# The large mixtures of a two-network kernel: experts' rows combined in SBUF by a 0/1 matrix, shared weights loaded in halves

## The chip, the core and the metric

The kernel runs on one core of a Trainium2 chip. The metric is the device time of one execution in microseconds; lower is better. TensorE, VectorE (DVE), ScalarE (ACT), GpSimd (POOL) and the sync engine (SP) run instruction streams of their own and wait for each other on semaphores; 16 DMA engines move data between HBM and SBUF.

## What is computed

512 tokens of 1024 features pass through three blocks, each a mixer and a mixture of experts. The first mixture has 16 experts (MoE0). The second and third (MoE1, MoE2) are the large ones: 64 experts with weights of 1024x256, 1024x256 and 256x1024 in f32, of which each token uses two, and a shared expert of width 512 for all tokens:

```python
def hier_moe(h, w_rg, b_rg, w_re, b_re, w_gate, w_up, w_down, ws_gate, ws_up, ws_down, w_sg):
    """Top-1 group, then top-2 experts inside the group; plus gated shared expert."""
    ...
    gate = jax.nn.softmax(top_v, axis=-1) * p_sel[:, None]
    eid = g_sel[:, None] * EXPERTS_PER_GROUP_2 + top_i
    ...
        hid = jax.nn.silu(xb @ w_gate[e]) * (xb @ w_up[e])
        return hid @ w_down[e]
    ...
    y = jnp.zeros((N, D), xt.dtype).at[tok_sorted].add(out[dest] * gate_sorted[:, None])
    ys = (jax.nn.silu(xt @ ws_gate) * (xt @ ws_up)) @ ws_down
    y = y + jax.nn.sigmoid(xt @ w_sg) * ys
```

Behind it stands `x = x + gt2 * rmsnorm(y, ...)`, and then the next mixer or the output.

## The kernel before

The program is written engine by engine in stages: MoE0, a convolution mixer, MoE1, a gated delta network (gdn), MoE2. A mixture is `moe_sp`, `moe_pe`, `moe_ve`, `moe_ac` and `moe_gp`, one function for each engine, and the order in them is the order on the engine.

**Units.** A large mixture does 16 units (`m.NS`) of 4 experts with 32 rows each, 128 rows in all; up to 8 further units take the overflow of experts with more than 32 tokens (`overflow`, with branches on a count). In this run MoE1 has no overflow unit and MoE2 one. For unit n: `gather_gp` fetches the tokens' rows from `xn_d` in HBM; `turn_pe` transposes them (8 transposes), `turn_ve`/`turn_ac` write them to SBUF with the modulation; `gate_up_pe` multiplies by gate and up weights (64 matmuls of 256 columns, 128 records in the trace); `hidden_pe` transposes the product; `down_pe` multiplies by the down weights (16 matmuls of 512 columns). `down_ve` and `down_ac` copy a half each to `YB`, and ScalarE's queue stores the 128 rows of 4 KB to `y_d` in HBM (L2005). After the last unit GpSimd gathers each token's two rows from `y_d` (8 gathers, L2105), and `mix` scales and adds them to the shared expert's output `SO`.

**The loop on TensorE** for n = 0 to 15: gate and up of unit n, hidden of n-1, transposes of n+1, down of n-1, then `m.rate` = 2 side steps (`next(more)`) of the shared expert: 4 matmuls of 128x512 a step.

**The loads.** SP's queue issues all weight loads (L295), 1 MB each, into slots: 0 to 7 are the ring, 8 to 14 lie in the arena. A load waits until what was in its slot is used. The order in the loop is down of n-1, gate of n+1, up of n+1, four loads each, so each group of four waits for the group two ahead of it in the ring. A down load waits for gate weights (`("ps", "gu", ...)`), an up load for down weights. At a mixture's start 14 slots are filled ahead; the third load, of the shared gate weights, waits in slot 8 for the projection before the mixture (`m.after`), and with it all behind it.

**Positions.** While VectorE routes (`route_ve`), TensorE does two small steps for it, `positions_pe` and `tokens_pe`, and then waits for the first gather.

## Time and profile before

| | |
|---|---|
| runs of the kernel before | 2825.89, 2830.32, 2833.78 us; median 2830.32 |
| span of the profiled execution | 2829.8 us |
| busy share: PE, PEld, DVE, ACT, POOL | 75%, 53%, 38%, 29%, 8% |
| loads on q1 | 625.04 MB, 59.1% of 16 engines |
| ACT's queue, q10 | 37.23 MB, 3.2% |
| row stores to `y_d` | 51 of 512 KB, median 8.5 us from issue to landing |
| gathers from `y_d` | 24 |
| MoE1 streams, MoE2 streams | about 1176 to 1676 us, 2268 to 2775 us |

The page gives one execution: busy time of each engine, the span in 40 slices with the granted TensorE clock and the transfer rate, the DMA queues, the chain that ended last, and the costliest groups of instructions. A stage is read from its own slices, since the shares are means over stages with different bounds. A TensorE record with "128*32 128x256" has 32 weight columns and a moving operand of 256 columns; one f32 matmul leaves two records. "second" is a tile of type fp32r, "ring" and "arena" hold f32. In a timeline the brackets say how long the engine had been idle and what ended that.

### The profile page before, as it was taken

To read this page: it belongs to the slowest core of one execution; us is meant where nothing else is said; L and a number is where in the kernel's file an instruction comes from. 1 tells how busy PE (TensorE), PEld (TensorE's weight loads), DVE (VectorE), ACT (ScalarE), POOL (GpSimd) and SP (SyncE) were. 2 spreads that over 40 slices of the span, in tenths; PEclk is the share of its full clock that TensorE was granted. 3 is DMA by queue.
4 is the path that set the end of the run, shared out by engine and by line. 5 is a ranking of instruction groups with operands and counts; after the bars stand their busy time and mean duration, and the time that the engine had idled before them with its cause. 6 is when DMAs were issued, how large, how long until landed. Compare 5 with 4: busy or idle time off the path is not lost. (4 is left out here: it accounts for less than half of the span.)

```text
span 2829.8 us, 41468 instructions
## 1 busy us (share of the span) xinstructions
PE 2130.7 (75%) x17466; PEld 1499.7 (53%) x17466; DVE 1081.7 (38%) x1714; ACT 821.3 (29%) x1345; POOL 214.9 (8%) x220
## 2 busy tenths in 40 slices
PE   5999998897994799576766545899988676667652
PEld 3877776795773688332333214677766532323221
DVE  3278877544223444410111016566545520011103
ACT  4177776322223423200000005344423310100101
POOL 2001000101101000100000000111110100000001
PEclk8999999988997899788888777999998798888776
DMA  8357765546983222899999983211112699999995
GB/s 312 126 191 235 237 225 194 79 156 206 335 322 138 94 91 79 350 412 394 412 413 409 413 315 115 60 46 41 44 46 75 235 401 412 413 413 415 403 404 210
DMA packets 218816, 698.20 MB, mean 247 GB/s; under 512 B 24365, under 2 KB 123382, under 8 KB 161782
## 3 DMA queue, kind: packets, MB, share of 16 engines
q1 hardware_dynamic: 195446, 625.04, 59.1%
q0 software_dynamic: 12992, 33.10, 3.4%
q10 hardware_dynamic: 10176, 37.23, 3.2%
q8 instruction: 144, 2.36, 0.3%
q14 instruction: 58, 0.48, 0.0%
HBM read 664.34 MB, written 45.11 MB: 251 GB/s over the span
## 5 line engine op out<-in xcount | busy, mean ns | idle before, releaser
L220 PE MATMUL PS<-ring,arena 128*32 128x256 f32 (+5 forms) x7488 | 797.8, 486 | 408.7 <-DMA ring<-in_moe_w_up 172.7
L220 PE MATMUL PS<-second 128*128 128x256 f32 (+1 forms) x4416 | 798.8, 340 | 34.3 <-DVE second L239 28.6
L220 PEld LDWEIGHTS PS<-ring,arena 128*32 128x32 f32 (+3 forms) x7488 | 413.4, 138 | 749.6 <-issue 585.8
L220 PEld LDWEIGHTS PS<-second 128*128 128x128 f32 x4416 | 671.5, 194 | 143.9 <-issue 30.5
L232 ACT ACTIVATE arena<-PS 128x512 f32<-128x512 f32 (+1 forms) x338 | 170.3, 504 | 1038.2 <-PE PS L220 889.8
L239 DVE TENSOR_TENSOR arena<-arena,PS 128x256 f32<-128x256 f32 (+1 forms) x83 | 43.5, 524 | 746.5 <-PE PS L220 745.5
L220 PE MATMUL PS<-arena 128*64 128x64 f32 (+8 forms) x1600 | 270.2, 358 | 36.1 <-DVE arena L239 17.2
L258 DVE COPY arena<-PS 128x512 f32<-128x512 f32 (+4 forms) x169 | 93.6, 554 | 391.7 <-PE PS L220 367.1
L220 PEld LDWEIGHTS PS<-arena 128*128 128x128 f32 (+5 forms) x1600 | 156.4, 168 | 154.8 <-issue 106.1
L232 ACT ACTIVATE arena<-PS,small 128x128 f32<-128x128 f32 (+1 forms) x212 | 99.6, 470 | 458.8 <-PE PS L228 451.4
L228 PE MATMUL PS<-ident,arena 128*128 128x128 f32 x919 | 133.6, 296 | 130.5 <-ACT arena L232 79.2
L232 ACT ACTIVATE arena<-arena 128x512 f32<-128x512 f32 (+5 forms) x239 | 169.0, 707 | 166.3 <-DVE arena L239 59.3
L239 DVE TENSOR_TENSOR second<-ring,second 128x1024 fp32r<-128x1024 f32 (+1 forms) x88 | 142.6, 1621 | 192.4 <-ACT second L232 187.4
L228 PEld LDWEIGHTS PS<-ident,arena 128*128 128x128 f32 x919 | 112.3, 152 | 162.3 <-ACT arena L232 81.9
L239 DVE TENSOR_TENSOR arena<-arena 128x512 f32<-128x512 f32 (+10 forms) x286 | 176.3, 616 | 34.1 <-ACT arena L232 16.7
L232 ACT ACTIVATE second<-ring 128x1024 fp32r<-128x1024 f32 (+1 forms) x88 | 120.5, 1370 | 214.6 <-PE PS L220 193.2
L2084 POOL DMA_INDIRECT arena<-xn_d,arena x51 | 52.8, 1035 | 960.0 <-PE PS L228 753.9
L246 DVE TENSOR_SCALAR arena<-PS,small 128x128 f32<-128x128 f32 (+1 forms) x212 | 87.9, 415 | 35.4 <-PE PS L228 26.8
L220 PE MATMUL PS<-ring 64*64 64x64 f32 (+3 forms) x1792 | 76.7, 232 | 11.6 <-DVE ring L239 9.4
L220 PEld LDWEIGHTS PS<-ring 64*64 64x64 f32 (+2 forms) x1792 | 70.3, 143 | 24.0 <-DVE ring L239 14.1
L266 POOL TENSOR_TENSOR arena<-arena 128x768 f32<-128x768 f32 (+2 forms) x31 | 47.6, 1535 | 385.0 <-DVE arena L246 236.2
L2105 POOL DMA_INDIRECT arena<-y_d,arena x24 | 26.4, 1100 | 375.5 <-ACTq L77 369.1
(158 smaller groups left out, 1105.9 us busy)
## 6 DMA issues: line engine op xcount, KB each, us to landing
ring<-in_moe_w_up SPq DMA_DIRECT2D x148, 1024.0 KB, 12.2
ring<-in_moe_w_down SPq DMA_DIRECT2D x148, 1024.0 KB, 11.1
ring<-in_moe_w_gate SPq DMA_DIRECT2D x142, 1024.0 KB, 11.0
ring<-in_ada_w SPq DMA_DIRECT2D x48, 1024.0 KB, 5.4
y_d<-arena ACTq DMA_DIRECT2D x51, 512.0 KB, 8.5
ring<-in_w_mod SPq DMA_DIRECT2D x24, 1024.0 KB, 6.3
ring<-in_gdn_in_w SPq DMA_DIRECT2D x32, 512.0 KB, 4.1
ring<-in_hg_w_in SPq DMA_DIRECT2D x24, 512.0 KB, 7.2
```

What stands on the lines that cost most here:

```text
L220: return P.e.matmul(o, l, r, start=st, stop=sp)
L228: return P.e.transpose(o, i, ident[:, :])
L232: A.e.activation(o, i, f, **kw).then_inc(*A.mark(*label))
L239: V.e.tensor_tensor(o, a, b, op).then_inc(*V.mark(*label))
L246: V.e.tensor_scalar(o, a, s1, s2, op0, op1).then_inc(*V.mark(*label))
L258: V.e.tensor_copy(o, a).then_inc(*V.mark(*label))
L266: G.e.tensor_tensor(o, a, b, op).then_inc(*G.mark(*label))
L2084: G.e.indirect_dma_start(out=XG[n % 3][0:m.G_ * m.C], out_offset=None, in_=xn_d, in_offset=bass.IndirectOffsetOnAxis(ap=m.idx[0:m.G_ * m.C ...
L2105: G.e.indirect_dma_start(out=m.ybuf[i], out_offset=None, in_=m.y_d, in_offset=bass.IndirectOffsetOnAxis(ap=m.yi[:, i // 2, i % 2:i % 2 + 1 ...
```

## The change

For MoE1 and MoE2 alone:

- `down_ac` scales unit n's rows by the tokens' gate values `m.ws` into `YP[0]`, rounded to fp32r; `down_ve` writes what the rounding left into `YP[1]`. `where_ve` makes the 0/1 matrix `WT`, rows to tokens. `combine_pe` multiplies both by it: 4 token tiles x 2 halves x 2 = 16 matmuls of 128x512. `combine_ve` adds the eight results to `XN` in SBUF (unit 0 copies). The side steps of the shared expert's down product add to `XN` too.
- The stores to `y_d`, the eight gathers behind the last unit, `mix` and the zero fill of 4 MB of `y_d` at the program's start go.
- `m.ws` and the token numbers come from more small work in routing (`shares_ve`, `shares_pe`, `columns_ve`).
- The shared gate and up weights come in eight halves of 0.5 MB each through slots 15 and 16. Four side steps stand ahead of the first unit; then a loop has one, loops 1, 3, 5 and 12 two. MoE1's ring starts at slot 0.
- Transposes of n+1 stand behind down of n-1. PSUM banks: six for units (0 to 4 and 7), 5 and 6 for the side steps.

```diff
-        for ne, c_, p in ((16, 128, 128), (64, 32, 128)):
+        for ne, c_, p in ((16, 128, 128),):
...
+    YP = [second[AR0 + 23040][:, 1024 * i:1024 * i + 1024] for i in range(2)]
+    WT = second[AR0 + 29184][:, :]
...
+    def piece_sp(m, q):
+
+        p, w, h = q // 4, q // 2 % 2, q % 2
+        src = m.shared[w][:, 256 * p:256 * p + 256].rearrange("(p h k) n -> p h k n", h=2, k=4)[:, h]
+        load(slots(15 + h), src, 4, ("ps", "sh", m.i, p, w, h), "sh", m.i, p, w, h, n=1024)
...
+    def begin_sp(m, turn):
+
+        free = ("ps", "cv", 11, 1) if m.i == 1 else ("ps", "rc", 7, 1)
+        state["slots"].update({12: free, 13: free, 14: ("sq2", m.before, 3), 15: m.after, 16: m.after, 9: None, 10: None})
+        expert_sp(m, slots(12), 0, 0, 0)
+        expert_sp(m, slots(13), 0, 0, 1)
+        for w, h in ((0, 2), (0, 3), (1, 0), (1, 1)):
+            expert_sp(m, turn, 0, w, h)
+        for q in range(2):
+            piece_sp(m, q)
+        for n, w, h in ((0, 1, 2), (0, 1, 3), (1, 0, 0), (1, 0, 1)):
+            expert_sp(m, turn, n, w, h)
+        S.wait_ge(at("xn_d", m.i), at("ps", "h2T", m.i, 3, 1))
+        expert_sp(m, slots(9), 1, 0, 2)
+        expert_sp(m, slots(10), 1, 0, 3)
+        expert_sp(m, slots(14), 1, 1, 0)
+        for q in range(2, 4):
+            piece_sp(m, q)
+        for h in range(1, 4):
+            expert_sp(m, turn, 1, 1, h)
...
         for n in range(m.NS):
+            if m.shared and n in (2, 3, 4, 6):
+                piece_sp(m, {2: 4, 3: 5, 4: 6, 6: 7}[n])
+            if m.shared and n in (5, 9):
+                if n == 5:
+                    state["slots"][11] = ("tokf2", m.i)
+                else:
+                    state["slots"][8] = ("ps", "sh", m.i, 1, 1, 1)
+                shared_down_sp(m, n // 9)
             if n:
...
-        S.wait_ge(at("comb", m.i, 7))
+        if m.shared:
+            S.wait_ge(at("ps", "cm", m.i, m.NB - 1, 3, 1))
...
+    def combine_pe(m, n):
+
+        P.wait_ge(at("W", m.i, n), at("ev", "down", m.i, n, 1))
+        for t in range(4):
+            for f in range(2):
+                b = take(state["units"], "cm", m.i, n, t, f)
+                for j in range(2):
+                    i = mm(b, WT[:, 128 * t:128 * t + 128], YP[j][:, 512 * f:512 * f + 512], j == 0, j == 1)
+                i.then_inc(*P.mark("ps", "cm", m.i, n, t, f))
...
-            for f in range(2):
-                for w in range(2):
-                    b, u = take(turn, "sh", m.i, p, f, w), unit("sh", m.i, p, w)
-                    P.wait_ge(at("ld", "sh", m.i, p, w))
-                    for k in range(8):
-                        P.wait_ge(at("h2", m.i, k))
-                        i = mm(b, u[:, k, f * 128:(f + 1) * 128], H2T[:, k, :], k == 0, k == 7)
-                        if k == 3:
-                            yield
-                    i.then_inc(*P.mark("ps", "sh", m.i, p, f, w))
-                    yield
+            for w in range(2):
+                b2 = [take(turn, "sh", m.i, p, w, f) for f in range(2)]
+                for h in range(2):
+                    u = unit("sh", m.i, p, w, h, k=4, n=1024)
+                    P.wait_ge(at("ld", "sh", m.i, p, w, h))
+                    for f, b in enumerate(b2):
+                        for k in range(4):
+                            P.wait_ge(at("h2", m.i, 4 * h + k))
+                            i = mm(b, u[:, k, f * 128:(f + 1) * 128], H2T[:, 4 * h + k, :], h + k == 0, h == 1 and k == 3)
+                        if f:
+                            i.then_inc(*P.mark("ps", "sh", m.i, p, w, h))
+                        yield
...
         more = shared_pe(m) if m.shared else iter(())
+        next(more, None)
         positions_pe(m)
+        next(more, None)
         tokens_pe(m, "tok", 0, m.NS)
+        for _ in range(2):
+            next(more, None)
         turn_pe(m, 0)
         for n in range(m.NS):
             gate_up_pe(m, n)
+            if m.shared and n == 0:
+                shares_pe(m, "share", m.NS)
             if n:
                 hidden_pe(m, n - 1)
-            if n + 1 < m.NS:
+            if m.shared is None and n + 1 < m.NS:
                 turn_pe(m, n + 1)
             if n:
                 down_pe(m, n - 1)
-            for _ in range(m.rate):
+            if m.shared and n + 1 < m.NS:
+                turn_pe(m, n + 1)
+            if m.shared and n:
+                combine_pe(m, n - 1)
+            for _ in range(side_steps(n)):
                 next(more, None)
             if n == 1:
                 tokens_pe(m, "tok2", m.NS, m.NB)
+                if m.shared:
+                    shares_pe(m, "share2", m.NV)
...
+        if m.shared:
+            combine_pe(m, m.NS - 1)
...
+        if m.shared:
+            for f in range(2):
+                V.wait_ge(at("ps", "down", m.i, n), at("hi", "y", m.i, n, f))
+                stt(YP[1][:, 512 * f:512 * f + 512], bank("down", m.i, n, f), m.ws[:, n:n + 1], YP[0][:, 512 * f:512 * f + 512].bitcast(f32),
+                    ALU.mult, ALU.subtract, "ev", "down", m.i, n, f)
+            return
...
+    def where_ve(m, n):
+
+        V.wait_ge(at("ps", "cm", m.i, n - 1, 3, 1) if n else None)
+        tt(WT.rearrange("p (t s) -> p t s", s=128), bc(iota[:, :].unsqueeze(1), 4, 128), bc(m.tokf[:, n, :].unsqueeze(2), 4, 128), ALU.is_equal, "W", m.i, n)
+
+    def combine_ve(m, n):
+
+        for t in range(4):
+            for f in range(2):
+                o, b = XN[:, t, 512 * f:512 * f + 512], bank("cm", m.i, n, t, f)
+                V.wait_ge(at("ps", "cm", m.i, n, t, f))
+                if n:
+                    tt(o, b, o, ALU.add, "ev", "cm", m.i, n, t, f)
+                else:
+                    cp(o, b, "ev", "cm", m.i, n, t, f)
...
             for n in range(2):
+                o = XN[:, t, n * 512:(n + 1) * 512]
                 V.wait_ge(at("ps", "sd", m.i, t, n))
-                ts(SO[:, t, n * 512:(n + 1) * 512], bank("sd", m.i, t, n), m.sgate[:, t:t + 1], None, ALU.mult, None, "ev", "sd", m.i, t, n)
+                stt(o, bank("sd", m.i, t, n), m.sgate[:, t:t + 1], o, ALU.mult, ALU.add, "ev", "sd", m.i, t, n)
...
             if n:
                 hidden_ve(m, n - 1)
-            if n + 1 < m.NS:
+            if m.shared is None and n + 1 < m.NS:
                 turn_ve(m, n + 1)
             if n:
                 down_ve(m, n - 1)
+            if m.shared and n + 1 < m.NS:
+                turn_ve(m, n + 1)
+            if m.shared and n:
+                combine_ve(m, n - 1)
+                where_ve(m, n)
...
+        if m.shared:
+            for f in range(2):
+                A.wait_ge(at("ps", "down", m.i, n), at("ps", "cm", m.i, n - 1, 3, 1) if n else at("ev", "share", m.i), at("ev", "share2", m.i) if n >= m.NS else None)
+                act(YP[0][:, 512 * f:512 * f + 512], bank("down", m.i, n, f), ACT.Copy, "hi", "y", m.i, n, f, scale=m.ws[:, n:n + 1])
+            return
...
+            A.wait_ge(at("ev", "cm", m.i, m.NB - 1, t, 1) if m.shared else at("mix", m.i, t))
...
+        if m.shared:
+            fill(RTY[:, 0:1], 0.0, "passed", m.i)
+            return
...
-        moe_sp(MO[1], slots(4, 5, 6, 7, 0, 1, 2, 3))
+        moe_sp(MO[1], slots(0, 1, 2, 3, 4, 5, 6, 7))
```

The sync queue at MoE1's start, before. `arena` and `ring` are where a load goes:

```order
212 L295 DMA ring<-in_conv_out_w 128x8x256 x4
213 L295 DMA arena<-in_moe_w_gate 128x2048 x2
214 L295 DMA arena<-in_shared_w_gate 128x8x256
215 L295 DMA ring<-in_moe_w_gate 128x2048
216 L295 DMA ring<-in_moe_w_up 128x2048 x4
217 L295 DMA ring<-in_moe_w_gate 128x2048 x3
218 L295 DMA arena<-in_moe_w_gate 128x2048
```

The same place now:

```order
212 L295 DMA ring<-in_conv_out_w 128x8x256 x4
213 L295 DMA arena<-in_moe_w_gate 128x2048 x2
214 L295 DMA ring<-in_moe_w_gate 128x2048 x2
215 L295 DMA ring<-in_moe_w_up 128x2048 x2
216 L295 DMA arena<-in_shared_w_gate 128x4x256 x2
217 L295 DMA ring<-in_moe_w_up 128x2048 x2
218 L295 DMA ring<-in_moe_w_gate 128x2048 x2
219 L295 DMA arena<-in_moe_w_gate 128x2048 x2
```

Four loads of expert weights have moved ahead of the first one of shared weights.

TensorE in a loop of MoE1 before: down of one unit, side steps, gate and up, hidden with transposes:

```order
353 L220 MATMUL PS<-ring,arena 32x512 x16
354 L220 MATMUL PS<-arena 128x512 x8
355 L220 MATMUL PS<-ring,arena 32x256 x64
356 L228 MATMUL PS<-ident,arena 128x128 x10
357 L220 MATMUL PS<-ring,arena 32x512 x16
```

And now, a loop with one side step and one with two ("second" are the matrix and the scaled rows):

```order
384 L228 MATMUL PS<-ident,arena 128x128 x2
385 L220 MATMUL PS<-ring,arena 32x512 x16
386 L228 MATMUL PS<-ident,arena 128x128 x8
387 L220 MATMUL PS<-second 128x512 x16
388 L220 MATMUL PS<-arena 128x512 x4
389 L220 MATMUL PS<-ring,arena 32x256 x64
390 L228 MATMUL PS<-ident,arena 128x128 x2
391 L220 MATMUL PS<-ring,arena 32x512 x16
392 L228 MATMUL PS<-ident,arena 128x128 x8
393 L220 MATMUL PS<-second 128x512 x16
394 L220 MATMUL PS<-arena 128x512 x8
```

Between down and the next gate weights stand eight transposes, 16 new matmuls and one or two side steps in place of two. On VectorE, one loop now:

```order
796 L258 COPY arena<-PS 128x256
797 L250 SCALAR_TENSOR_TENSOR second<-PS,arena,second 128x512 x2
798 L246 TENSOR_SCALAR arena<-PS,small 128x128 x4
799 L239 TENSOR_TENSOR arena<-PS,arena 128x512 x8
800 L239 TENSOR_TENSOR second<-iota,arena 128x512
801 L239 TENSOR_TENSOR arena<-arena,PS 128x256
```

The two subtractions stand where one copy of 128x512 stood, and eight additions and the matrix behind them are new.

## Rows read from the trace of the kernel before

**Rows 1.** The windows view: us of each engine, granted clock, DMA share, GB/s.

```profile
1140.00:1165.00 25.00, 3.54 (x29) 2.66 (x29) 16.80 (x52) 7.47 (x13) 3.99 (x3) 0.57 0.97 379
...
1176.00:1660.00 484.00, 313.61 (x2702) 148.65 (x2703) 65.13 (x142) 46.44 (x96) 11.90 (x12) 0.84 1.00 408
2268.00:2740.00 472.00, 305.14 (x2650) 143.88 (x2648) 62.62 (x134) 44.62 (x92) 11.86 (x12) 0.84 1.01 410
```

**Rows 2.** DMA view, 1180 to 1660 us: packets, MB, share of 16 engines.

```profile
q1 hardware_dynamic: 29647, 185.13, 94.7%
q10 hardware_dynamic: 2016, 7.34, 3.7%
```

**Rows 3.** The same view, 2270 to 2740 us.

```profile
q10 hardware_dynamic: 2016, 7.34, 3.8%
```

**Rows 4.** Timeline of TensorE, one loop of MoE1: start, us, instructions.

```profile
1406.26 5.23 PE L220 MATMUL PS<-ring,arena 128*32 128x512 f32 x32 [3.61 <-DMA ring<-in_moe_w_down]
1411.42 7.13 PE L220 MATMUL PS<-arena 128*128 128x512 f32 x16
1418.48 3.66 PE L220 MATMUL PS<-ring,arena 128*32 128x256 f32 x64
1428.48 6.06 PE L220 MATMUL PS<-ring,arena 128*32 128x256 f32 x64 [6.34 <-DMA ring<-in_moe_w_up]
```

**Rows 5.** Timeline of the sync queue in the same loop.

```profile
1411.55 1.75 SPq L295 DMA_DIRECT2D ring<-in_moe_w_up  x4
1422.21 1.75 SPq L295 DMA_DIRECT2D ring<-in_moe_w_down  x4
```

**Rows 6.** Timeline of TensorE at 1744 us, a price.

```profile
1744.48 5.70 PE L220 MATMUL PS<-second 128*128 128x512 f32 x24
```

**Rows 7.** VectorE groups by form, behind 1080 us: busy us, mean ns.

```profile
L239 DVE TENSOR_TENSOR arena<-PS,arena 128x512 f32<-128x512 f32 x24 | 16.6, 692 | 18.0 <-PE PS L220 16.7
...
L250 DVE SCALAR_TENSOR_TENSOR arena<-PS,cols,arena 128x512 f32<-128x512 f32 x8 | 6.0, 751 | 5.0 <-PE PS L228 4.4
```

**Rows 8.** A ScalarE group by form, behind 1080 us.

```profile
L232 ACT ACTIVATE arena<-PS 128x512 f32<-128x512 f32 x95 | 56.8, 598 | 447.2 <-PE PS L220 367.6 <-DVE ring L239 62.2 <-DVE arena L239 8.7
```

**Rows 9.** DMA view, 1408 to 1428 us, slices of 0.5 us.

```profile
GB/s 418 410 451 377 426 418 451 426 393 442 360 344 360 393 393 287 311 418 418 451 426 418 426 459 402 410 459 426 393 393 410 475 426 393 426 442 426 442 410 442
```

**Rows 10.** Timeline of the sync queue at MoE1's start.

```profile
1076.09 0.81 SPq L295 DMA_DIRECT2D arena<-in_moe_w_gate  x2
1122.97 0.60 SPq L295 DMA_DIRECT2D arena<-in_shared_w_gate  x1
...
1172.13 0.33 SPq L295 DMA_DIRECT2D ring<-in_moe_w_gate  x1
```

**Rows 11.** DMA view, 1084 to 1174 us, slices of 2.25 us.

```profile
GB/s 0 7 4 0 0 0 0 7 0 0 0 0 0 0 7 0 0 9 218 345 405 428 426 426 417 424 430 422 419 433 426 401 353 354 317 191 59 106 0 62
```

**Rows 12.** Timeline of TensorE at MoE1's start.

```profile
1152.44 0.59 PE L220 MATMUL PS<-arena 128*128 128x16 bf16 x16 [4.79 <-DVE arena L239]
1162.32 1.97 PE L228 MATMUL PS<-ident,arena 128*128 128x128 f32 x8 [9.29 <-DMA arena<-xn_d,arena]
```

**Rows 13.** Timeline of all engines behind MoE1's last unit.

```profile
1678.28 5.75 PE L220 MATMUL PS<-ring,arena 128*32 128x512 f32 x32 [6.84 <-SPq L77]
...
1684.82 0.33 ACTq L2005 DMA_DIRECT2D y_d<-arena  x1
...
1721.33 6.43 PE L228 MATMUL PS<-ident,arena 128*128 128x128 f32 x32 [37.30 <-ACT arena L232]
```

**Rows 14.** Timeline of all engines at the end of MoE2.

```profile
2790.36 3.64 PE L220 MATMUL PS<-ring,arena 128*32 128x512 f32 x32 [2.71 <-SPq L77]
...
2794.78 0.33 ACTq L2005 DMA_DIRECT2D y_d<-arena  x1
...
2825.54 1.22 DVE L239 TENSOR_TENSOR arena<-arena 128x1024 f32<-128x1024 f32 x1
```

**Rows 15.** Timeline of TensorE during the zero fills.

```profile
52.19 23.12 PE L220 MATMUL PS<-second 128*128 128x256 f32 x144 [11.13 <-DVE second L239]
```

More of the change, by code:

```diff
@@ L294, in load @@
             S.wait_ge(at(*before))
-        S.e.dma_start(unit(*label, k=k), src).then_inc(*state["ring"][slot_of[label]].next("ld", *label))
+        S.e.dma_start(unit(*label, k=k, n=n), src).then_inc(*state["ring"][slot_of[label]].next("ld", *label))
     def cols_of(w, c0):
@@ L2041, in moe_ac @@
                 tables()
-            if n + 1 < m.NS:
+            if m.shared is None and n + 1 < m.NS:
                 turn_ac(m, n + 1)
@@ L2045, in moe_ac @@
                 down_ac(m, n - 1)
-            for _ in range(m.rate):
+            if m.shared and n + 1 < m.NS:
+                turn_ac(m, n + 1)
+            for _ in range(4 * (n == 0) + side_steps(n)):
                 next(more, None)
```

161 lines of the change are left out of this document (89 added, 72 removed).

## The prediction

> **What bounds the kernel now.** I read the windows view first, then the DMA view of the same stretches, then one loop of the timeline. MoE1 streams its expert weights from 1176 to 1660 us, MoE2 from 2268 to 2740 us: 956 us, a third of the program. In both the 16 DMA engines are busy for a share of 1.00 and 1.01, while TensorE has work for 314 of 484 us and VectorE for 65 [rows 1]. The reader is to see that the transfers are the bound there: an engine's work costs time only if it makes the transfers stop. What fills the transfers is, in MoE1, 185.13 MB of loads (94.7%) and 7.34 MB on the ScalarE queue, q10, which are the row stores to `y_d` [rows 2]; MoE2 has the same 7.34 MB [rows 3].
>
> One loop shows how the ring of weights turns. The down weights of a unit land and TensorE starts on them at 1406.26, does two side steps of the shared expert (7.13 us), then the next gate weights at 1418.48; the up weights are not there before 1428.48 [rows 4]. The next load of down weights goes out at 1422.21, when the gate weights are used up, and the up loads at 1411.55, when the down weights are [rows 5]. So this load is issued 6.3 us before the last transfer ahead of it lands. That lead is what the change spends.
>
> **1. The row stores go.** Their time on the 16 engines is 3.7% of 480 us = 17.8 us in MoE1 [rows 2] and 3.8% of 470 us = 17.9 us in MoE2 [rows 3]. Behind a full queue this comes back whole: -35.7 us. A store also disturbs the loads: round the one issued at 1412.3 seven slices of 0.5 us fall from some 420 to a mean of 350 GB/s [rows 9]. That is 3.5 us x 70 GB/s = 245 KB, 0.58 us of transfer. I take 0.5 us for each of the 28 stores that 2 x 7.34 MB make at 0.52 MB: -14 us (between 0, if the dip is chance, and -16).
>
> **2. The start of each large mixture.** The two gate loads at 1076.09 are followed by a shared load that waits for the output projection until 1122.97 [rows 10]; the DMA stands still between [rows 11]. Now four ring loads stand ahead of it, in slots 0 to 3, which the projection's weights leave earlier. That alone gives nothing: the slots are full in either case and the transfers stop near 1162 us, until the first gate weights are used and 1172.13 issues the next load [rows 10, 11]. Two things move. 15 MB instead of 14 are in before that stop (the halves in slots 15 and 16 are used and loaded again): 1.05 MB at 408 GB/s = 2.6 us. And the first unit comes earlier: TensorE has almost nothing to do from 1140 to 1165 us (3.54 us, granted clock 0.57) [rows 1], its transposes wait 9.29 us for a gather [rows 12] that shares the engines with late loads. Four side steps of 3.6 us now stand in this gap. They raise the clock to 2.4 GHz before the first gate weights, which ran partly at 1.2 GHz; but they may also hold up the transposes if they run at 1.2 GHz themselves (4 x 7.1 us in 23 us). I take 4.4 us earlier, bounds 0 and 6. Together -7 us for each mixture: **-14 us**. MoE2's start has the same pieces.
>
> **3. The loop.** New for each unit: two ScalarE copies at 0.60 us [rows 8], two VectorE subtractions at 0.75 us and eight additions at 0.69 us [rows 7], the 0/1 matrix (0.69 us by the same row), and 16 matmuls of 128x512 on TensorE at 5.70 / 24 = 0.24 us = 3.8 us [rows 6]. VectorE has some 10 us of work in a loop of 31 us; it isn't the bound. On TensorE the combination stands ahead of the gate weights whose slots the next down load wants, and this wait is the one that matters. Its release moves by: one side step less, -3.6; eight transposes moved behind the down weights, +1.1; the wait for the scaled rows, 0.6 + 2 x 0.75 + gaps = +2.3; the combination, +3.8. Sum +3.6 us. What it has to be ahead of, the landing at 1428.48, comes 1.24 + 0.5 = 1.7 us earlier without the store. Of 6.3 us of lead 1.0 is left, about what lies between an issue and its first packets (loads issued from 1122.97 appear in the slice that starts at 1124.5 [rows 10, 11]). So a loop with one side step just keeps the queue full. Loops 1, 3, 5 and 12 have two steps: +3.6 us, of which a half of shared weights (0.5 MB, 1.3 us), loaded just ahead, covers a part in three of them. They run dry for 2.3, 2.3, 2.3 and 3.6 us, and the first has 1 us more of small matmuls for the overflow places. Down weights that run at 2.4 GHz all through (the other case is 5.23 us [rows 4]) give some of it back. I take 11 us for a mixture: **+22 us**, bounds 0 and, if the single-step loops miss too by 1.5 us, +55.
>
> On the half loads the Trainium skill speaks against the change: "DMA: Bandwidth & Descriptors", section "Bandwidth", asks for at least 1 MiB in a DMA (1 MB alone took 6.15 us there, 16 MB 79 us, so some 1.2 us of start each). By that, an estimate, 8 more starts in two mixtures would cost about 10 us. The trace shows 1 MB loads, one behind the other, at 408 GB/s with all engines busy [rows 1], so starts overlap, and I count nothing.
>
> **4. The end of each large mixture.** In MoE1 the last down matmuls end at 1684.0; store, gathers and mixing follow, and the next stage's transposes start at 1721.33 [rows 13]: 37.3 us. Now: scaled rows +2.4; eight additions behind the matmuls, +6.3; then norms that ScalarE bounds, four tokens' tiles of some 4.9 us less what overlaps, until +28 us. -9 us. In MoE2 the last matmuls end at 2794.0 and the span at 2829.8 [rows 14], 35.8 us. Now 8.7 us to the last addition, four tiles of post work at 2.6 us, 3 us for the output, with a slower clock about 24.5 us: -11. But its one overflow unit now waits behind unit 15's combination, +2. Together **-18 us**, bounds -10 and -24.
>
> **5. At nothing:** the second zero fill at 52 us goes (4.2 MB), but TensorE works through 23.12 us without a gap beside both [rows 15]. The routing vectors that VectorE adds ahead of unit 0 (some 3 us) lie in the wait for gathers and first matmuls; if the gate weights' evacuation becomes late, that is 1 us for a mixture.
>
> **The sum.** -35.7 - 14 - 14 + 22 - 18 = -59.7 us. The profiled execution has 2829.8 us of span, within 1 us of the median 2830.32, so it needs no correction: **2770 us**.
>
> **Rival A: the queue never runs dry.** The lead in [rows 5] is large enough because down weights often find TensorE at the high clock. Then +22 falls away: 2748 us. For it: only four loops have two steps. Against it: 1.0 us of lead is thin.
>
> **Rival B: the single-step loops miss too**, by 1.5 us in each of 22: +33 us, 2803 us. For it: the dependence down, scale, combine, side step, gate has four hand-overs between engines that I priced without queues, and eight banks pass through six slots, so the last two matmul pairs wait for VectorE's first additions.
>
> **Rival C, slower: the combination runs at the low clock.** TensorE waits 3.61 us for the down weights, which then take 5.23 us, against 3.6 when warm [rows 4]. If the new wait for scaled rows keeps it at 1.2 GHz through combination and side step, these cost 3.8 + 3.6 us more in a loop. The lead is gone, and 28 loops run dry by some 5 us more: 2770 + 140 = 2910 us at the worst; with the side step at full speed 28 x 3.8 = 106, 2876 us, which I take as its time. It decides from 82 / 28 = 2.9 us of dry queue in every loop. Against it: 7.13 us for 16 records behind the cold down weights is the full rate [rows 4]; the clock is back by then, and a pause of 2.4 us follows a burst of 6. The Trainium skill has this as a rule ("TensorE: Matmul & The Clock Gate", section "HAM oscillation"): bursts with waits for DMA between them start cold each time. By that rule, the trace agrees for the down weights and not for what stands behind them.
>
> **Rival D: the early loads aren't early**, since slots 0 to 3 are released late, or side steps hold up the transposes: part 2 gives nothing, 2784 us.
>
> **Chances.** Forecast 0.55, A 0.17, B 0.13, C 0.07, D 0.08. The range reaches to A and B with their bounds: 2743 to 2808 us. About 0.3%, 8.5 us, is what a measurement can tell from no change. Faster by more: forecast, A, D and nearly all of B, 0.88; within it 0.05 (B where it is worse); slower 0.07 (C).
>
> **What would show it.** In the changed profile: q10 almost empty in the streaming stretches, and these shorter by 15 to 25 us at a DMA share of 0.98 or more; the down load's issue within 2 us of the up weights' landing in single-step loops, and gaps of 2 to 4 us in four loops; 16 matmuls of 128x512 in 3.8 us (7.6 says rival C); the first gate weights 3 to 5 us earlier after the routing; and 28 us instead of 37 between the last down matmuls and the next stage. A DMA share under 0.93 in the loops would make the prediction wrong to the slow side.

## The result, and the profile after

The changed kernel takes 2864.31 us (median of 4 runs, 2857.81 to 2868.47) against 2829.6 us for the kernel before: a ratio of 1.0113, with a 95% interval of 1.009 to 1.0137. It is slower by 35 us, where the prediction had 60 us less. Its profiled execution has a span of 2865.0 us.

The windows view of the changed kernel, in the columns of [rows 1]:

```profile
1176.00:1660.00 484.00, 331.94 (x2804) 167.07 (x2808) 162.65 (x282) 54.94 (x107) 13.93 (x14) 0.87 0.94 381
2268.00:2740.00 472.00, 328.60 (x2854) 168.23 (x2858) 158.05 (x280) 54.06 (x104) 14.92 (x15) 0.86 0.91 370
```

The DMA share was 1.00 and 1.01 [rows 1] and is 0.94 and 0.91. These are the streaming stretches, and no engine is near its limit in them (TensorE 332 of 484 us, VectorE 163). So the transfers stop and wait. The DMA view from 1180 to 1660 us shows that the stores are gone, since there is no q10 any more (it had 3.7% [rows 2]):

```profile
q1 hardware_dynamic: 29757, 179.09, 91.6%
q0 software_dynamic: 1728, 3.13, 1.7%
```

In the same time 179 MB of loads come in, where 185 did before. The place they had been given free was not used. TensorE's waits from 1176 to 1660 us (engine, line, what it waited for: us, times, longest), first before:

```profile
PE PS L220 <- DMA ring<-in_moe_w_up: 86.5, 15, 6.9
PE PS L220 <- DMA ring<-in_moe_w_down: 59.2, 14, 10.0
```

and after:

```profile
PE PS L220 <- DMA ring<-in_moe_w_down: 107.9, 14, 12.2
PE PS L220 <- DVE second L250: 21.1, 14, 1.9
PE PS L220 <- DMA ring<-in_moe_w_up: 17.8, 8, 3.4
```

The wait has moved from the up weights to the down weights, and that names the load that comes late. A loop with one side step, and after it one with two (loop 12), on TensorE:

```profile
1542.04 5.40 PE L220 MATMUL PS<-ring,arena 128*32 128x512 f32 x32 [8.68 <-DMA ring<-in_moe_w_down]
1547.37 1.09 PE L228 MATMUL PS<-ident,arena 128*128 128x128 f32 x8
1549.94 4.19 PE L220 MATMUL PS<-second 128*128 128x512 f32 x16 [1.48 <-DVE second L250]
1553.96 3.60 PE L220 MATMUL PS<-arena 128*128 128x512 f32 x8
1557.49 3.66 PE L220 MATMUL PS<-ring,arena 128*32 128x256 f32 x64
1564.55 3.66 PE L220 MATMUL PS<-ring,arena 128*32 128x256 f32 x64 [3.40 <-DMA ring<-in_moe_w_up]
...
1574.74 6.11 PE L220 MATMUL PS<-ring,arena 128*32 128x512 f32 x32 [6.17 <-DMA ring<-in_moe_w_down]
```

and on the sync queue:

```profile
1561.21 2.02 SPq L295 DMA_DIRECT2D ring<-in_moe_w_down  x4
...
1598.06 2.02 SPq L295 DMA_DIRECT2D ring<-in_moe_w_down  x4
```

The DMA view around the second of these issues, 1588 to 1608 us in slices of 0.5 us:

```profile
GB/s 426 426 410 442 410 426 426 426 459 328 213 164 82 16 0 0 0 0 0 0 0 0 82 180 377 442 459 377 426 459 410 426 426 459 426 377 426 492 393 410
```

The queue drains from 1592.5, stands empty from 1595 to 1599, and fills again about 1 us after the issue at 1598.06. Against 420 GB/s this is 6.3 us without transfer. In the text below the **dry time** of a loop is this sum around the issue of the down loads, and **x** is the time from the start of the last down matmuls to that issue: 1598.06 - 1574.74 = 23.3 us here, 19.2 us in the loop ahead of it, and 1422.21 - 1406.26 = 15.95 us before [rows 4, 5].

Where the 35 us lie, by the starts of the down matmuls (down(n) is that of unit n; after less before):

| stretch | MoE1 | MoE2 |
|---|---|---|
| up to down(0) (in MoE2: from the next stage's start) | -7.7 | -3.5 |
| down(0) to down(14), 14 loops | +18.8 | +23.9 |
| down(14) to down(15) | +6.8 | +7.0 |
| down(15) to the overflow unit's down | no such unit | +4.3 |
| last down to the next stage or the end | -7.1 | -7.3 |

### The profile page after: what moved, and what is told of

It is laid out like the page before. It is cut to its first block and busy times, and to the rows that moved or that the text cites. A ratio compares the mean times of both kernels' runs of the same rounds, so it can differ in the third digit from the quotient of the medians.

```text
span 2865.0 us, 43231 instructions
## 1 busy us (share of the span) xinstructions
PE 2246.7 (78%) x18058; PEld 1589.9 (55%) x18058; DVE 1303.3 (45%) x2046; ACT 846.6 (30%) x1378; POOL 194.2 (7%) x205
## 5 line engine op out<-in xcount | busy, mean ns | idle before, releaser
L220 PE MATMUL PS<-second 128*128 128x256 f32 (+1 forms) x4944 | 940.9, 348 | 89.7 <-DVE second L250 54.6
L220 PE MATMUL PS<-ring,arena 128*32 128x256 f32 (+4 forms) x7424 | 750.8, 459 | 326.6 <-DMA ring<-in_moe_w_down 239.8
L220 PEld LDWEIGHTS PS<-second 128*128 128x128 f32 x4944 | 767.9, 195 | 242.4 <-DVE second L250 65.8
L220 PEld LDWEIGHTS PS<-ring,arena 128*32 128x32 f32 (+3 forms) x7424 | 389.0, 129 | 641.3 <-issue 474.3
L220 PE MATMUL PS<-arena 128*64 128x64 f32 (+8 forms) x1728 | 302.5, 360 | 37.9 <-ACT arena L232 18.7
L220 PEld LDWEIGHTS PS<-arena 128*128 128x128 f32 (+4 forms) x1728 | 178.8, 173 | 142.3 <-issue 81.3
L250 DVE SCALAR_TENSOR_TENSOR second<-PS,arena,second 128x512 fp32r<-128x512 f32 x66 | 49.5, 751 | 440.0 <-ACT second L232 422.3
L239 DVE TENSOR_TENSOR arena<-PS,arena 128x512 f32<-128x512 f32 x281 | 193.9, 690 | 72.5 <-PE PS L220 46.3
L232 ACT ACTIVATE second<-PS,arena 128x512 fp32r<-128x512 f32 x66 | 45.4, 687 | 594.1 <-PE PS L220 593.0
L239 DVE TENSOR_TENSOR arena<-arena 128x512 f32<-128x512 f32 (+9 forms) x290 | 177.4, 612 | 34.2 <-ACT arena L232 16.7
## 6 DMA issues: line engine op xcount, KB each, us to landing
ring<-in_moe_w_up SPq DMA_DIRECT2D x146, 1024.0 KB, 10.1
```

Source lines behind the costliest of these rows:

```text
L220: return P.e.matmul(o, l, r, start=st, stop=sp)
L232: A.e.activation(o, i, f, **kw).then_inc(*A.mark(*label))
L239: V.e.tensor_tensor(o, a, b, op).then_inc(*V.mark(*label))
L250: V.e.scalar_tensor_tensor(o, a, s, b, op0, op1).then_inc(*V.mark(*label))
```

## The experiments

**Theory 1**, from the traces: combination and side steps stand on TensorE ahead of the gate weights whose slots the next down loads want, so the queue runs dry in every loop. Its rivals: TensorE's own chain makes the loop whatever the order; the low clock does; VectorE's additions do; the stores never cost what the prediction took back for them.

**side_behind**: the side steps behind the gate weights (the new argument of `gate_up_pe` is called between its gate and its up matmuls).

```
-            gate_up_pe(m, n)
+            gate_up_pe(m, n, lambda: sides(n - 1) if m.shared and n else None)
...
-            for _ in range(side_steps(n)):
-                next(more, None)
```

> The changed kernel with one thing moved: the side steps of the shared expert stand between the gate and the up matmuls of the next unit, no longer ahead of both. Theory 1 (the combination and the side steps stand ahead of the gate weights whose slots the next down loads need, so the queue of loads runs dry in each loop): the down loads go out 3.6 us earlier in loops with one side step and 7.2 us in those with two. The changed kernel's loops of 33.0 us should fall to about 30 us, which is 12 MB at 425 GB/s (29.6 us) and little else, those of 36 to 38 us to 30 or 31: about 28 x 3 + 8 x 3 = 100 us less, 2770 us. Rival 2 (a loop is as long as TensorE's own chain, since the same work stands between two units whatever its order): nothing changes, 2865 us. Rival 3 (the DMA queue moves bytes more slowly now because of half loads): loops of 33 us stay, and only the deep dips shrink, 2840 us.

Measured: 2826.6 us, 0.9988 of before (0.9973 to 1.0003), 38 us less than the changed kernel. Order matters, so rival 2 falls, and loops of 31 us with the same half loads leave nothing for rival 3. But the gain is a little over a third of what was forecast, and it is uneven: later in MoE1 most loops take 30.3 to 32.6 us where they took 33 to 36, but the first five still 35 to 38. Sync queue and TensorE in one of these:

```profile
1346.20 2.02 SPq L295 DMA_DIRECT2D ring<-in_moe_w_up  x4
1361.06 0.38 SPq L295 DMA_DIRECT2D arena<-in_shared_w_up  x1
1361.48 1.93 SPq L295 DMA_DIRECT2D ring<-in_moe_w_down  x4
```

```profile
1353.73 3.66 PE L220 MATMUL PS<-ring,arena 128*32 128x256 f32 x64 [0.90 <-DVE arena L239]
1357.32 3.70 PE L220 MATMUL PS<-arena 128*128 128x512 f32 x8
```

The gate weights were used up at 1357.4, but the down loads are issued 4 us later. Ahead of them on SP stands a piece of the shared weights whose slot a side step has to free, and this step is now behind the gate weights. The order on one engine had been moved past the order on another.

**gate_first**: all of it behind the gate weights.

```
+        def behind(n):
+            if n:
+                combine_pe(m, n - 1)
+            for _ in range(side_steps(n)):
+                next(more, None)
...
-            gate_up_pe(m, n)
+            gate_up_pe(m, n, lambda: behind(n - 1) if m.shared and n else None)
```

> The changed kernel with the gate matmuls of the next unit directly behind the down matmuls, then the combination, the side steps and the up matmuls; the transposes of the next unit stand ahead of the down matmuls again, as in the kernel before, and the combination has two PSUM banks of its own. Theory 1 (the queue runs dry because the next down loads wait for gate weights that stand behind the combination): the down loads go out some 9 us before the up weights land, more lead than the 6.3 us of the kernel before; the DMA share returns to 0.99 or more in the streaming stretches, loops are 29.6 to 30.5 us; 2755 us, between 2740 and 2775. Rival 2 (TensorE's own chain): 2865 us. Rival 4 (two banks make the combination wait for VectorE's eight additions of 0.78 us, so it ends behind the landing of the up weights and the up loads of the following unit come late instead): 2790 to 2820 us.

Measured: 2904.6 us, 1.0253 (1.0214 to 1.0292): slower by 40 us than the changed kernel, where 110 less were forecast. The most instructive miss. TensorE in a loop behind the shared pieces:

```profile
1581.65 6.08 PE L220 MATMUL PS<-ring,arena 128*32 128x256 f32 x64 [10.22 <-DMA ring<-in_moe_w_gate]
1587.66 1.20 PE L220 MATMUL PS<-second 128*128 128x512 f32 x4
1589.17 4.71 PE L220 MATMUL PS<-second 128*128 128x512 f32 x12 [0.32 <-DVE arena L239]
1593.72 3.59 PE L220 MATMUL PS<-arena 128*128 128x512 f32 x8
1597.25 3.66 PE L220 MATMUL PS<-ring,arena 128*32 128x256 f32 x64
```

The down loads go out early here (1587.79). But the up weights wait behind gate, combination and side step until 1600.9, and it is their slots that the next gate loads want, so the queue is dry from 1599 to 1603. That costs 3 us there, and it is not what made this run slow. The fault of side_behind is here too, and larger, since the step that frees a shared slot now stands behind gate and combination. Sync queue and TensorE in such a loop:

```profile
1379.67 0.38 SPq L295 DMA_DIRECT2D arena<-in_shared_w_up  x1
1380.09 2.00 SPq L295 DMA_DIRECT2D ring<-in_moe_w_down  x4
```

```profile
1364.74 5.32 PE L220 MATMUL PS<-ring,arena 128*32 128x256 f32 x64 [4.83 <-DMA ring<-in_moe_w_gate]
```

The gate weights are used up at 1370.1 and the down loads go out 10 us later. Five loops of each mixture are like this one (those whose down loads stand behind a shared load that waits for a side step); they take 40.1 to 44.8 us, together 66 us more than in the changed kernel, and the other 18 loops together 19 us less. So where nothing holds the sync queue, the order of this run is the better one. There are three groups of loads in a loop and two halves of a ring: each group waits for the use of the one two places ahead, and work that is taken from before one is put before the next. I had looked at one group alone.

**half_sum**: half of the combination's matmuls.

```
-                for j in range(2):
-                    i = mm(b, WT[:, 128 * t:128 * t + 128], YP[j][:, 512 * f:512 * f + 512], j == 0, j == 1)
+                i = mm(b, WT[:, 128 * t:128 * t + 128], YP[0][:, 512 * f:512 * f + 512], True, True)
```

> The changed kernel with half of the combination: only the rounded part of the scaled rows is multiplied, 8 matmuls for a unit instead of 16, so the sums lack their small parts. It leaves out 2.1 us of TensorE's time ahead of the gate weights in each of the 32 loops and nothing else. Theory 1: every loop is dry by over 2.1 us, so each gets shorter by that, 28 to 31 loops x 2.1 = 59 to 65 us, 2803 us. Rival 5 (VectorE's eight additions of 6.3 us, not TensorE, hold the chain, through the banks): under 10 us, 2855 to 2865 us.

Measured: 2857.7 us, 1.0096 (1.0064 to 1.0127), where the changed kernel has 1.0113 (1.009 to 1.0137): under 10 us less, as rival 5 has it, and not resolved from nothing. TensorE in one combination of this run:

```profile
1551.35 1.20 PE L220 MATMUL PS<-second 128*128 128x512 f32 x4 [1.48 <-DVE second L250]
1553.20 1.29 PE L220 MATMUL PS<-second 128*128 128x512 f32 x3 [0.66 <-DVE arena L246]
1554.80 0.50 PE L220 MATMUL PS<-second 128*128 128x512 f32 x1 [0.30 <-DVE arena L239]
1555.13 3.60 PE L220 MATMUL PS<-arena 128*128 128x512 f32 x8
```

Eight matmuls take 1551.35 to 1555.30, 3.95 us, and sixteen took 4.19. The PSUM banks come free at the pace of VectorE, which first has 1.75 us of copies of the transposes to do. For 32 units the 0.24 us make 7.7 us, which the times allow and do not show. The count of matmuls is not what this step costs.

**no_stores**: the kernel before, without its row stores.

```
-        A.e.dma_start(m.y_d[128 * n:128 * n + 128, :], YB[n % 2])
+        r0, r = (128 * (n % 8), 1) if m.shared else (128 * n, 128)
+        A.e.dma_start(m.y_d[r0:r0 + r, :], YB[n % 2][0:r, :])
```

> The kernel before without the large mixtures' row stores: the same store instruction carries one row of 4 KB instead of 128 rows, and the gathers at the end read rows of zeros, so the experts' outputs are left out of the result. Nothing else is changed. It measures step 1 of the prediction alone. Prediction: the stores' time on the engines comes back whole, 35.7 us, and the dips around them, 14 us: 2780 us, loops shorter by 1.7 us each. Rival: only the transfer, 2794 us. Rival: the stores ride beside the loads for nothing, 2830 us, in which case the change never had this gain to spend.

(The rest of the edit makes the gathers read rows of zeros and keeps the zero fill at its size.)

Measured: 2800.6 us, 0.9892 (0.9862 to 0.9922), 29 us less, between 22 and 39. The transfer's 35.7 us lie in the interval. The 14 us for the dips around the stores do not: that part of step 1 was not there to be gained.

What the first four runs left was the question how the work has to stand, and how much lead the queue needs.

**balanced**: down(n-1), side steps, gate(n+1), combination(n-1), up(n+1).

```
-            gate_up_pe(m, n)
+            gate_up_pe(m, n, lambda: combine_pe(m, n - 2) if m.shared and n > 1 else None)
...
-                b = take(state["units"], "cm", m.i, n, t, f)
+                b = take(state["sums"], "cm", m.i, n, t, f)
```

> The changed kernel with TensorE's order in a loop: down(n-1), side steps, gate(n+1), combination(n-1), up(n+1), and the transposes ahead of down; combination in two PSUM banks of its own. What the runs before taught: side steps behind the gate weights gained 1 to 2 us in single-step loops but held SP, which waits for a side step before it loads the next piece of shared weights, ahead of the down load; and with all of it behind the gate weights the gate loads came late instead, since the up weights stood behind 10 us of work. Theory 1b (each of the three groups of loads needs its slots used about 3.5 us before the group ahead of it has landed for TensorE, and only an even spread of the work gives all three this): side steps in the pause before the gate weights land, combination in the pause before the up weights. Down load out some 6 us ahead, gate load 6 us, up load 4 us. Loops of 30.5 us, DMA share 0.98 or more: 2770 us, between 2755 and 2790. Rival 4b (the combination, paced by VectorE's eight additions through two banks, ends behind the landing of the up weights, and the gate loads come late by 1 to 2 us in each loop): 2810 us. Rival 2 (order does not matter): 2860 us.

Measured: 2797.9 us, 0.988 (0.9843 to 0.9916). Windows view and one loop:

```profile
1176.00:1660.00 484.00, 372.92 (x2989) 176.44 (x2989) 172.45 (x297) 58.67 (x112) 13.92 (x14) 0.91 0.98 401
2268.00:2740.00 472.00, 365.82 (x2840) 170.95 (x2838) 167.41 (x272) 53.43 (x101) 11.04 (x12) 0.90 0.98 400
```

```profile
1522.48 4.96 PE L220 MATMUL PS<-ring,arena 128*32 128x512 f32 x32 [5.03 <-DMA ring<-in_moe_w_down]
1527.37 3.70 PE L220 MATMUL PS<-arena 128*128 128x512 f32 x8
1534.62 5.35 PE L220 MATMUL PS<-ring,arena 128*32 128x256 f32 x64 [3.55 <-DMA ring<-in_moe_w_gate]
1539.89 1.20 PE L220 MATMUL PS<-second 128*128 128x512 f32 x4
1541.40 4.71 PE L220 MATMUL PS<-second 128*128 128x512 f32 x12 [0.31 <-DVE arena L239]
1546.04 3.66 PE L220 MATMUL PS<-ring,arena 128*32 128x256 f32 x64
```

The reader is to see that the pauses are now spread (5.0, 3.6 and 0.3 us, where the changed kernel has 8.7, 1.5 and 3.4), and that the DMA share is back at 0.98. The same matmuls, additions and loads as in the changed kernel, 66 us less: the change was sound, and the order that it gave to TensorE was not. It is 28 us above the forecast of 2770 and 8 above its upper bound. Rival 4b has a part in that: in the loop shown the last up load lands at 1544.39, the combination holds the up matmuls until 1546.04, and after the next gate loads went out late (1549.77) the DMA rate dips for 0.9 us. How much of the 28 us this makes was not measured.

**balanced_tail**: the same, with down(15) ahead of combination(14).

> The same with one thing more: the down matmuls of the last unit (15) stand ahead of the combination of unit 14. In the changed kernel 19.0 and 17.6 us lie between the down matmuls of units 14 and 15, against 12.3 and 10.6 before; the trace shows that down(14), scaled rows, combination, side step and transposes of hidden fill them, not the transfer. Theory: this gap returns to some 11 us in both mixtures, 7 us each, of which the combination of 14 behind down(15) gives a part back, since it is VectorE's additions that end the mixture: 2 x 4 us = 8 us less than the run without it. Rival: all of it is given back behind down(15), 0 us.

Measured: 2792.3 us, 0.9845 (0.9803 to 0.9886). From down(14) to down(15) it is 10.1 and 10.0 us where it was 17.0 and 17.7, so the gap was TensorE's chain. But the work has only moved: in MoE1 the next stage comes 42.9 us behind down(15) instead of 36.0, and in MoE2 the overflow unit's down 37.9 us instead of 32.1. That takes back all of it in MoE1 and most of it in MoE2, near to what the rival said. The total is 5.5 us lower, which the intervals of the two runs do not separate. This version beats both kernels.

**warm_down and warm_six**: 12 and 6 matmuls for nothing ahead of the wait for the down weights.

```
+        if m.shared and n < m.NS - 1:
+            for j in range(12):          # 6 in warm_six
+                mm(b2[0], ident[:, :], H2T[:, j % 8, :], True, True)
```

> The changed kernel with 12 matmuls of 128x512 that compute nothing used, ahead of the wait for the down weights, about 5.4 us of work in a pause of 8 to 10 us. They shall keep TensorE's clock up: the down matmuls take 5.0 to 6.6 us in the changed kernel and 3.6 at full speed. Rival C of the prediction (the low clock is what costs): down in 3.6 to 4.5 us, the gate weights used 2 us earlier, the dips of the queue shorter by that in all loops: 2810 us. Theory 1 says the same of this step, since for it too the chain is what counts, but expects a part of it alone where TensorE falls back in the rest of the pause: 2810 to 2850. If the chain through down does not bound the loops: 2865 us.

Measured: 2893.2 us, 1.0209 (1.0171 to 1.0247), 29 us more than the changed kernel. The twelve took 10.5 us and not 5.4, for an fp32 matmul of 128x512 takes 0.88 us and leaves two records; I had read 0.45 for it from a row that counts records. They ended behind the landing of the down weights. The down matmuls of the 32 units in question ran in 3.6 us, but too late. The run says nothing on the rival, so it was made again with six:

> The changed kernel with 6 matmuls that compute nothing used ahead of the wait for the down weights, in place of 12, which took 10.5 us and so longer than the pause. Six take 5.3 us of a pause of 6 to 9. Theory 1c: if down then runs in 3.6 to 4.5 us instead of 5.0 to 6.6, the down loads go out 1 to 2.2 us earlier after it; each dip gets shorter by this until it is gone: 28 x 1.5 = 40 us less, 2820 us. If the pause that is left after the six lets the clock fall again, down stays at 5 us and over, and the time at 2860. The same if the extra matmuls themselves run at the low clock and end behind the landing.

Measured: 2845.4 us, 1.0045 (1.0026 to 1.0064), 19 us less than the changed kernel. In 22 of 33 units the down matmuls take 3.6 us, in the others over 5. TensorE in one loop:

```profile
1439.37 3.64 PE L220 MATMUL PS<-ring,arena 128*32 128x512 f32 x32 [1.54 <-DMA ring<-in_moe_w_down]
...
1468.69 5.39 PE L220 MATMUL PS<-arena,ident 128*128 128x512 f32 x12 [0.79 <-DVE arena L258]
1474.13 3.64 PE L220 MATMUL PS<-ring,arena 128*32 128x512 f32 x32
```

In 5 of MoE1's 16 units the six themselves end behind the landing, as at 1474.1, where down has no wait ahead of it; this takes away a part. So the low clock of the down matmuls has some 20 us in it, half of what Theory 1 gave to it. It is a length in the chain that makes the down loads late, not a cause beside it: in balanced most down matmuls still take 5.0 to 6.5 us, and the queue stays full.

**no_stores_late and no_stores_late4**: the kernel before without stores, with 9 and 4 extra matmuls ahead of the gate weights. No new wait, no work on VectorE: only the release is later.

```
+        if m.shared and 1 < n < m.NS:
+            for j in range(9):           # 4 in no_stores_late4
+                mm(b2[0], ident[:, :], XGT[n % 2][:, 0:4, :].rearrange("p k s -> p (k s)"), True, True)
```

> The kernel before without the large mixtures' row stores (experts' outputs left out, as in the run of that name) and with 9 matmuls of 128x512 that compute nothing used ahead of the gate weights of units 2 to 15: about 4.1 us later release of the gate slots, from some 6 us of lead to some 2, with no new wait and no work on VectorE. It asks how much lead the queue needs. The prediction's step 3 took about 1 us as enough: 2801 us, as without them, with a few us for the loop of the routers. Theory 1b (3.5 us are needed): 1 to 2 us dry in each of 28 loops: 2830 to 2850 us.

Measured: 2926.3 us, 1.0326 (1.0287 to 1.0364). The nine took 7.9 us, twice their price, as above. This run gave the line, which was then put to the test with four (3.5 us):

> The kernel before without the large mixtures' row stores, as in the run of that name, and with 4 extra matmuls of 128x512 in place of the 9 of the last such run, whose matmuls took 0.88 us each, twice what I had priced. In all runs so far the dry stretch of the queue near a down load's issue follows one line: the time from the start of the last down matmuls to this issue, less 17.3 us. Theory 1c (that line): 16.1 + 3.5 = 19.6 us, so 2.3 us dry in each of 11 loops of both mixtures, and 0 in the loops without side steps: about 2800 + 48 = 2848 us, loops of 33 us where they were 31. The prediction's step 3 (about 1 us between the issue and the landing ahead of it is enough, so 5 us of spare): 2801 us.

Measured: 2845.8 us, 1.0036 (1.0018 to 1.0053), against 2848 by the line and 2801 by the prediction's step. x and the dry time, from the timelines and the slices of the DMA view, loops without loads for the router or the shared expert:

| kernel | x, us | dry, us | x - 17.3 |
|---|---|---|---|
| before, two side steps and no combination | 15.3 to 17.4 | 0 | below 0.1 |
| balanced, but for one loop | 13.5 to 17.5 | 0 to 0.5 | below 0.2 |
| side_behind, later loops | 16.4 to 17.9 | 0 to 1.2 | below 0.6 |
| after, one side step | 18.8 to 20.2 | 0.6 to 3.3 | 1.5 to 2.9 |
| no_stores_late4 | 19.5 to 20.7 | 2.3 to 3.7 | 2.2 to 3.4 |
| after, loops 10 (row) and 12 (two steps) | 23.0 to 23.3 | 5.1 to 6.2 | 5.7 to 6.0 |
| no_stores_late | 23.7 to 25.0 | 6.5 to 8.4 | 6.4 to 7.7 |

Past 17.3 the line holds within 1.5 us in these six kernels, two of which have neither a combination nor a new wait. So a later use of the gate weights is enough by itself to empty the queue, and this is shown, not argued. Two neighbouring loops can differ by 2 us at one x. A part of that is the gathers: over 58 loops past the line (after, balanced, no_stores_late4, no_stores_late), the dry time stands 0.2 us above it on the mean where the other queues move under 0.3 MB in the loop's x, and 0.7 us below it where they move 0.3 MB or more, as it should be if these bytes keep the engines busy longer. The rest is open.

The line asks that the gate and up loads ahead went out in time. The one loop of balanced that was left out (loop 6, x = 19.1, 0.3 us dry) had its dip of 0.7 us ahead of that, at the gate loads, and in gate_first x reaches 20 with 0.2 us dry, since there the loop waits for the gate weights. In warm_six, where the extra matmuls can hold the down matmuls behind their landing, x starts too late, and the dry time is up to some 2 us above the line.

**row_behind**: the one row step (loop 10) moved behind the gate weights.

```
-            if n == m.row_at:
+            if n == m.row_at and m.shared is None:
                 row_pe(DIAG, ("row", m.i), state["side"])
```

> The changed kernel with the one row step (the mixture's gate row, loop 10: 2.2 us of TensorE and a wait of 1.3 us for VectorE's additions) moved from ahead of the gate weights to between the gate and the up weights. The prediction had counted nothing for this step, which the change moves from loop 4 to loop 10. Theory 1c: the down load of this loop goes out 3.6 us earlier, its dip falls from 5.4 to 2 us, in both mixtures: 7 us less, 2858 us. If such a step costs nothing: 2865 us.

Measured: 2861.8 us, 1.010 (1.0069 to 1.0131). In the trace the loop does what was said (x 23.3 to 19.9, interval 35.7 to 32.3 us in MoE1, 35.6 to 32.6 in MoE2), but a total of 7 us less is not resolved: inconclusive for the sum, and as forecast for the loop.

## Why the prediction was wrong

**What held.** The DMA bound of both stretches. The size of part 2: down(0) of MoE1 comes 7.7 us earlier against 7 forecast, in MoE2 3.5, so 11 of 14. In MoE1 half of this is luck. The first unit was to come 4.4 us earlier, yet its transposes start at 1162.21 us, as before (1162.32 [rows 12]), and its gate weights 1.0 us earlier (1165.32 against 1166.35). What moved down(0) is that TensorE ran the unit at a granted clock of 1.00 instead of 0.57 (1162 to 1172 us) and that three of its four down loads went out from 1172.85 on instead of 1187.08. The end of the mixtures: from the end of the last down matmuls -5.0 and -8.7 us, against -9 and -11, so 14 of 20 with the same mechanism; the gathers are gone, and eight additions and the norms bound what is left. The zero fill at nothing. And of the loop, the release of the gate slots: +3.6 us was forecast, on the 15.95 us of [rows 4, 5], so x = 19.55; measured were 18.8 to 20.2. Copies in place of 0.60 took 0.70 us, the combination 4.19 in place of 3.8, and both came out in the sum.

**The step that failed: how much lead the queue needs (part 3).** I took the 6.3 us from the issue at 1422.21 to the start of the up matmuls at 1428.48 as lead, took off 1.7 us for the store, and 1.0 us as what must be left of it, "about what lies between an issue and its first packets". That left 3.6 us to spend, and the change needed all of them. The line says that from x = 17.3 the queue runs dry: from 15.95 only 1.35 us were to be spent. The 1.0 us was right: in queues that had run empty, 0.96 us pass from the issue to the first packet. Missing was the other end: TensorE's start is not the end of the transfer. In the loop shown above a dip of the loads has its lowest slice from 1562.5 to 1563.0 and the up matmuls start at 1564.55:

```profile
GB/s 434 401 434 377 459 410 393 459 377 459 442 279 377 49 344 426 377 508 377 393 475 360 459 426 393 459 442 344 475 377 442 459 360 475 442 377 492 426 377 492
```

(the changed kernel, 1556 to 1576 us). The packets of 61 loops that ran dry (after, half_sum, no_stores_late4, no_stores_late) show what this time is. The 16 engines do not finish together, as the slices from 1592.5 to 1595 above show. If the lost transfer time of this tail is put together, the queue ends 1.65 us (median; 0.8 to 3.3) ahead of the landing of the last up load, though the very last packet ends only 0.43 us ahead of it, and TensorE starts 0.14 us behind it. So 1.8 us at this end look free on a timeline of TensorE and are not; they are most of the 2.25 us between 3.6 and 1.35. This also gives the line, as an estimate: behind the down weights stand eight loads of 1.05 MB, 20.0 us at 420 GB/s, and 20.0 - 1.8 - 1.0 = 17.2 us, where 17.3 was read.

The Trainium skill has a cost at this end in "DMA: Bandwidth & Descriptors", section "Anatomy of one DMA — SWDGE (gpsimd) path": about 2.0 us of fixed cost in each DMA issued by GpSimd, most of it the receipt of the last write ahead of the semaphore. These loads are issued by SP, and their 0.43 us from last packet to landing do not agree with so long a receipt; the measurement decides. I had used the same page to weigh half loads.

What it made: 0.6 to 3.3 us dry in the single-step loops without other loads, where I had none (with a shared load ahead of the down load most lose 0.1 to 0.4 us), and 3.5 to 7 in those with two, where I had 2.3 to 3.6. Summed over 1180 to 1670 us of MoE1, dips of over 0.4 us take some 39 us more than before, where I had 11. Down(0) to down(14) was to become 14 us shorter in each mixture and became 18.8 and 23.9 us longer: 71 of the 94 us between forecast and result, of which some 21 are the stores' term below.

**A step left out.** The row step moved from loop 4 to loop 10, where it waits 1.3 us for VectorE's additions: x 23.3 and 23.2, 5.4 and 5.1 us dry. The change's own line (`row_at`) said so, and I counted nothing. Its net price is open: before, loop 4 of MoE1, which held the row step, was dry for 3.2 us (x = 24.0), that of MoE2 not at all.

**A term too small: the last unit (part 4).** I had 2 us for a unit that waits behind a combination. Down(15) starts 6.8 and 7.0 us later behind down(14), the overflow unit 4.3 more: 18 us. TensorE there:

```profile
1677.09 6.14 PE L220 MATMUL PS<-ring,arena 128*32 128x512 f32 x32 [8.46 <-DMA ring<-in_moe_w_down]
1685.73 5.45 PE L220 MATMUL PS<-second 128*128 128x512 f32 x16 [2.50 <-DVE second L250]
1691.01 3.60 PE L220 MATMUL PS<-arena 128*128 128x512 f32 x8
1694.44 0.38 PE L228 MATMUL PS<-ident,arena 128*128 128x128 f32 x2
1696.13 3.64 PE L220 MATMUL PS<-ring,arena 128*32 128x512 f32 x32 [1.31 <-DVE arena L258]
```

No DMA is waited for between the two downs: 6.1 + 2.5 + 5.5 + 3.6 + 0.4 + 1.3 us of chain stand where 12.3 us had been a transfer. balanced_tail shows it by closing the gap, though the work that it moved took the time back further on.

**A term too large: the stores (part 1).** 49.7 us forecast, 29 (22 to 39) measured alone. The seven low slices of [rows 9] were read from one store and multiplied by 28.

**The rivals.** B had the right mechanism, single-step loops that miss too, at 1.5 us each; it would have needed more in each, the last units, and less for the stores, and its 2803 us are 61 short. C had the right sign, and its 2876 us are the nearest number, 12 us off, by luck: its reason did not come. Its combination did not run at the low clock (4.19 us, where 7.6 was to show it), and warm_six puts the clock at some 20 us in all; but its break-even of 2.9 us dry in a loop was about reached, at 2.8 us more than before in MoE1 and 3.1 in MoE2. Of the signs that I had named, the one for the slow side came in MoE2: a DMA share of 0.91, under 0.93; MoE1 has 0.94.

## What to carry to other kernels

Where loads stream through a ring, write down for each group of loads the last use that frees its slots and every load ahead of it on the issuing queue, and count its lead to where the transfer rate falls in the DMA view, not to the start of the engine that waits for the data: here 1.8 us at that end and 1.0 us at the issue looked free and were not. New work on an engine that has 170 us idle still belongs into its pauses, and each pause takes only what fits; the same instructions cost 1.1% in one order and gave 1.2% in another. Before multiplying a price by a count of records, divide one record's time: an fp32 matmul leaves two.

## What had not been expected of the hardware

- The lead that this queue of 1 MB loads needs is a line. Past it the dry time grows about one for one: 3.5 us of extra matmuls in 28 loops made 20 of them 2.3 to 3.7 us dry and cost 45 us, 7.9 us made them 5.8 to 8.4 us dry and cost 126.
- The end of a drained queue is ragged: with its tail put together it ends 1.65 us ahead of the landing of the last load, its last packet 0.43 us ahead (medians of 61 loops).
- An fp32 matmul of 128x512 takes 0.88 us at full clock (12 in 10.5 us); the fp32r one 0.26 (16 in 4.19, with waits for banks).
- ScalarE's copy with a scale into fp32r takes 0.70 us for 128x512 (1.41 for two), against 0.60 for the plain one [rows 8].
- Eight VectorE additions from PSUM set the pace of the matmuls that feed them: 6.26 us for eight, and with two banks (gate_first, balanced) the sixteen matmuls take 6.2 us, with six banks 4.2.
